# A fourth split buffer through the experts of a two-layer decoder trunk, with a new order for the last down tiles and the picks

## The reference

```python
logits = (ht @ w_router).astype(jnp.float32)
top_vals, top_idx = lax.top_k(logits, TOP_K)          # TOP_K = 2 of 8
top_w = jax.nn.softmax(top_vals, axis=-1)
...
for e in range(N_EXPERTS):
    y = swiglu(ht, w_gu[e], w_down[e], D_FF_EXPERT)    # D_FF_EXPERT = 1792
    out = out + combine[:, e:e + 1] * y.astype(jnp.float32)
```

## Time and profile before

| | us |
|---|---|
| median of 3 runs | 1234.74 |
| lowest and highest | 1233.70, 1234.78 |
| the profiled execution, its own time | 1234.06 |
| its span in the trace | 1232.2 |
| PE busy | 1213.9 (99%) |
| DVE busy | 899.6 (73%) |
| ACT busy | 721.4 (59%) |
| mean granted PE clock | 0.994 |

### The profile page before, as it was taken

One profiled execution on the slowest core, in us unless ns is written; L12 is line 12 of the kernel. 1 busy time (PEld: TensorE's weight loads), 2 busy tenths in 40 slices (PEclk: granted clock), 3 DMA queues, 4 the chain that ended last, 5 costly groups with the idle time before them and its releaser, 6 DMA issues.

```text
span 1232.2 us, 15422 instructions
## 1 busy us (share of the span) xinstructions
PE 1213.9 (99%) x6004; PEld 1012.5 (82%) x6004; DVE 899.6 (73%) x864; ACT 721.4 (59%) x677; POOL 110.7 (9%) x131
## 2 busy tenths in 40 slices
PE   9999999999999999999999999999999999999997
PEld 7997787788888888998788878888888888888876
DVE  5777755654544467667756668999898888888996
ACT  5346544534343446435644377777777777777765
POOL 4600000200000001330000100000010001000301
PEclk9999999999999999999999899999999999999999
DMA  9955454655555546655445389999999999999970
GB/s 299 318 172 171 139 181 158 232 179 198 178 198 179 198 153 212 190 169 177 155 167 185 137 296 373 373 385 378 386 382 380 388 384 384 382 390 379 391 280 35
DMA packets 152204, 317.55 MB, mean 258 GB/s; under 512 B 6273, under 2 KB 41345, under 8 KB 152146
## 3 DMA queue, kind: packets, MB, share of 16 engines
q1 hardware_dynamic: 147328, 302.27, 69.9%
q0 software_dynamic: 4112, 13.44, 3.0%
q10 hardware_dynamic: 706, 1.07, 0.3%
HBM read 310.99 MB, written 5.77 MB: 257 GB/s over the span
## 4 chain that ended last, share of the span: by engine, by line
PE 89%; DVE 6%; ACT 3%; issue 2%; POOLq 0%; POOL 0%; ACTq 0%; DVEq 0%
PE ps L1804 23%; PE ps L1549 16%; PE ps L1551 16%; PE ps L1550 16%; PE ps L1791 11%; DVE split L975 2%; ACT split L629 2%; PE ps L1771 1%; PE ps L1565 1%; PE ps L1586 1%; PE ps L1639 1%; DVE hT L1007 1%; PE ps L1665 1%; PE ps L1760 1%; PE ps L1694 0%
## 5 line engine op out<-in xcount | busy, mean ns | idle before, releaser
L975 DVE TENSOR_TENSOR split<-raw,split 128x2048 fp32r<-128x2048 f32 x279 | 639.2, 2295 | 231.2 <-ACT split L629 228.5
L629 ACT ACTIVATE split<-raw 128x2048 fp32r<-128x2048 f32 x279 | 534.4, 1916 | 262.7 <-PE ps L1551 192.9
L1804 PE MATMUL ps<-split,br 128*128 128x512 f32 x1344 | 317.7, 393 | 1.5 <-DVE br L1097 1.0
L1804 PEld LDWEIGHTS ps<-split,br 128*128 128x128 f32 x1344 | 249.4, 188 | 56.2 <-issue 2.1
L1549 PE MATMUL ps<-split,hT 128*128 128x512 f32 (+1 forms) x600 | 235.4, 392 | 3.2 <-DVE hT L1007 1.9
L1551 PE MATMUL ps<-split,hT 128*128 128x512 f32 (+1 forms) x600 | 230.5, 384 | 0.0
L1550 PE MATMUL ps<-split,hT 128*128 128x512 f32 (+1 forms) x600 | 230.3, 384 | 0.0
L1791 PE MATMUL ps<-split,hT 128*128 128x512 f32 x672 | 159.6, 392 | 0.1
L1791 PEld LDWEIGHTS ps<-split,hT 128*128 128x128 f32 x672 | 124.8, 188 | 27.9 <-issue 1.6
L1549 PEld LDWEIGHTS ps<-split,hT 128*128 128x128 f32 x600 | 112.8, 188 | 29.0 <-DVE hT L1007 3.6
L1551 PEld LDWEIGHTS ps<-split,hT 128*128 128x128 f32 x600 | 112.7, 188 | 22.6
(11 more groups left out here) (267 smaller groups left out, 990.3 us busy)
## 6 DMA issues: line engine op xcount, KB each, us to landing
raw<-moe_w_gu_dram SPq DMA_DIRECT2D x96, 1024.0 KB
raw<-moe_w_down_dram SPq DMA_DIRECT2D x56, 1024.0 KB
raw<-w_in_dram SPq DMA_DIRECT2D x45, 1024.0 KB
raw<-ffn_w_gu_dram SPq DMA_DIRECT2D x28, 1024.0 KB
raw<-moe_w_gu_dram SPq DMA_DIRECT2D x32, 512.0 KB
raw<-ffn_w_down_dram SPq DMA_DIRECT2D x14, 1024.0 KB
raw<-w_branch_dram SPq DMA_DIRECT2D x12, 1024.0 KB
raw<-w_out_dram SPq DMA_DIRECT2D x8, 1024.0 KB
```

The source lines that it names most:

```text
L629: act.activation(buffer(t, 0), raw[:, t % RAW, :], ACT.Copy).then_inc(hi, 1)
L975: dve.tensor_tensor(buffer(t, 1), raw[:, t % RAW, :], buffer(t, 0).bitcast(F32), ALU.subtract).then_inc(lo, 1)
L1804: ins = pe.matmul(ps[:, 5 if kind == "up" else 4, :], xe[:, sl, 4 * part + k, :], slot(t, sr, 512)[:, k, :], start=part + k + m == 0, stop ...
```

## The change

1. From the first tile of the embedding projection of layer 1 on (`LAST_RING`), the split ring has four buffers to the end; every fourth tile goes to the rows of `br`. Since 21 tiles are no multiple of 4, an expert's buffers are no longer those of the one before, and PE's loop over the experts is written out.
2. ACT and DVE split two tiles ahead as before up to step 9 of expert 1, two and three ahead in step 10 (`AT_AHEAD`), and three ahead from there. In step 18 of every expert, the split now stands behind the eviction of the tail.
3. The four picks go to four buffers (two of them the free `qT` and `kT`), issued one after the other; DVE adds them at steps 9, 10, 12, 13.
4. In the last expert the three last down tiles are taken first for output columns 0 to 511 and then for 512 to 1023; the turn of the tail comes after the first six matmuls. The first half is scattered and added (`add_last(b, 0)`) ahead of the second half's low part, which now lies in `pT`. The third and fourth turn of `X` stand later in `quad`.
5. `weight_exp` moves from expert 0 to the routing, followed by a small silu on ACT.

```diff
+LAST_RING = LAYER_T0[1] + T_PROJ[1]
-AT_COMBINE = (8, 9, 13, 14)
+AT_COMBINE = (9, 10, 12, 13)
+AT_AHEAD = (1, 10)
...
         def buffers(t):
-            return SPLIT + 1 if 0 <= t - LAYER_T0[1] < EXTRA else SPLIT
+            return SPLIT + 1 if 0 <= t - LAYER_T0[1] < EXTRA or t >= LAST_RING else SPLIT
...
+        def lead(i, j):
+            tiles = (2,) if (i, j) < AT_AHEAD else (2, 3) if (i, j) == AT_AHEAD else (3,)
+            return [n for n in tiles if i < EXPERTS - 1 or j + n < BODY_TILES]
...
             def picks(s):
+                pool.wait_ge(picked, s)
                 for n, (b, k) in enumerate(((0, 0), (0, 1), (1, 0), (1, 1))):
-                    if n < 2:
-                        pool.wait_ge(picked, s)
-                    else:
-                        pool.wait_ge(picks_used, 4 * (s - 1) + n - 1)
-                    pool.indirect_dma_start(Y[:, n % 2, :], None, ye_rows[s][:, :], bass.IndirectOffsetOnAxis(
+                    pool.indirect_dma_start(pick_rows[n], None, ye_rows[s][:, :], bass.IndirectOffsetOnAxis(
...
             def expert(s, t0, i, last):          # ACT; DVE alike
-                    if not last or j + 2 < BODY_TILES:
-                        split_hi(t0 + j + 2, i, BODY_TILES, s)
-                    if s == 1 and i == 0 and j == 1:
-                        weight_exp()
+                    elif j != AT_LAST:
+                        for ahead in lead(i, j):
+                            split_hi(t0 + j + ahead, i, BODY_TILES)
...
                     if j == AT_LAST:
                         ...
                         if not last:
                             gather_hi(s, 1, 2 + i * 2)
+                        if s == 1:
+                            for ahead in lead(i, j):
+                                split_hi(t0 + j + ahead, i, BODY_TILES)
+                            if last:
+                                split_gate_hi(0)
...
                     store_y(1)
+                    weight_exp()
                     proj_out_of(1, 0)
...
                 if last and s == 1:              # DVE
                     for nh in range(2):
                         dve.wait_ge(ye_hi, nh + 1)
+                        dve.tensor_tensor(ye[nh][:, 1, :], ps[:, nh, :], ye[nh][:, 0, :].bitcast(F32),
                                           ALU.subtract).then_inc(ye_lo, 1)
+                        if nh == 0:
+                            add_last(0, 0)
+                            add_last(1, 0)
...
-                    add_last(0, 0)
-                    add_last(1, 0)
+                    turn_lo(7, (0, 1))
                     add_last(0, 1)
-                    turn_lo(7, (0,))
                     add_last(1, 1)
-                    turn_lo(7, (1,))
                     split_gate_lo(1)
...
+                def last_downs():                # PE
+                    pe.wait_ge(aT_lo[1], LAST_F + i * (LAST_F + 1))
+                    down_half(AT_LAST, 2, 0, 0)
+                    turn_act(1, LAST_F, i, True)
+                    pe.wait_ge(lo, t0 + AT_LAST + 2 + i * BODY_TILES)
+                    down_half(AT_LAST + 1, 2, 1, 0)
+                    pe.wait_ge(aT_lo[1], LAST_F + 1 + i * (LAST_F + 1))
+                    pe.wait_ge(lo, t0 + AT_LAST + 3 + i * BODY_TILES)
+                    down_half(AT_LAST + 2, LAST_F, 0, 0).then_inc(half_down[1], 1)
+                    for n in range(3):
+                        down_half(AT_LAST + n, 2 if n < 2 else LAST_F, n % 2, 1).then_inc(used, 1)
...
-                with pe.Fori(0, EXPERTS - 1) as e:
-                    expert(s, t0, e, False)
+                if s == 1:
+                    for e in range(EXPERTS - 1):
+                        expert(s, t0, e, False)
...
                 expert(s, t0, EXPERTS - 1, True)
+                if s == 1:
+                    pe.wait_ge(ye_lo, 1)
+                    for b in range(NB):
+                        scatter(b, 0)
...
                 if l:
                     last_turn(0, 1)
+                    pe.wait_ge(ye_lo, 2)
+                    for b in range(NB):
+                        scatter(b, 1)
...
-                     {(0, 0, 0, 0): lambda: last_turn(2), (0, 0, 1, 1): lambda: last_turn(3)} if l else
+                     {(0, 0, 1, 1): lambda: last_turn(2), (0, 1, 0, 1): lambda: last_turn(3)} if l else
```

More of the change, by code:

```diff
@@ L1156, in expert @@
                                           aT_moe[:, 0].bitcast(F32), ALU.subtract).then_inc(aT_lo[s], 1)
-                    if not last or j + 2 < BODY_TILES:
-                        split_lo(t0 + j + 2, i, BODY_TILES, s)
-                    elif s == 1 and j + 2 == BODY_TILES:
-                        split_gate_lo(0)
+                    if s == 2:
+                        if not last or j + 2 < BODY_TILES:
+                            split_lo(t0 + j + 2, i, BODY_TILES, s)
+                    elif j != AT_LAST:
+                        for ahead in lead(i, j):
+                            split_lo(t0 + j + ahead, i, BODY_TILES)
                     if s == 1 and i == 1 and j == AT_WEIGHTS[0]:
@@ L1172, in expert @@
                             gather_lo(s, 1, 2 + i * 2)
+                        if s == 1:
+                            for ahead in lead(i, j):
+                                split_lo(t0 + j + ahead, i, BODY_TILES)
+                            if last:
+                                split_gate_lo(0)
                     if last and s == 1 and j in AT_COMBINE:
@@ L1777, in expert, with tile, down_half @@
                 _, _, lo, used = STREAMS[s]
+                def tile(j, s_, n):
+                    return slot(t0 + j + (i * BODY_TILES if s == 1 else 0), s_, n)
+                def down_half(j, f, part, nh):
+                    for k in range(2):
+                        for m, (sl, sr) in enumerate(((0, 0), (0, 1), (1, 0))):
+                            lhs = aT_moe[:, sl, 2 * part + k, :] if f < LAST_F else aT_tail[:, sl, k, :]
+                            ins = pe.matmul(ps[:, nh, :], lhs, tile(j, sr, D)[:, k, cols(nh)],
+                                            start=f + part + k + m == 0, stop=f == LAST_F and k == 1 and m == 2)
+                    return ins
+                def last_downs():
[9 more added lines that the diff above has]
+                        down_half(AT_LAST + n, 2 if n < 2 else LAST_F, n % 2, 1).then_inc(used, 1)
                 for j, (kind, f, part) in enumerate(EXPERT_TILES):
@@ L1780, in expert @@
                     pe.wait_ge(lo, t + 1 + i * BODY_TILES)
+                    if last and s == 1 and j == AT_LAST:
+                        last_downs()
+                        break
                     if kind == "down":
@@ L1787, in expert @@
                         for nh in range(2):
[L1788 to L1794 removed]
+                            ins = down_half(j, f, part, nh)
                             if f == LAST_F and nh == 0:
```

61 lines of the change are left out of this document (30 added, 31 removed).

## The result

The changed kernel takes 1237.97 us at the median of 10 runs (1235.38 to 1240.71), the kernel before 1232.88 in the 10 runs that now stand beside it (1230.22 to 1234.78). The ratio is 1.0039 [1.0029, 1.0049]: slower by 0.4%, some 4.8 us. The forecast of 1237.0 and its range hold the time, but the sum behind it was +2.3, so half of the loss was not in it. That the total came so near is in part luck: it was built on a median of 1234.74 from three runs, and the ten runs of the same kernel give 1232.88. From there +2.3 would have given 1235.2. The profiled execution takes 1237.28 us, its span 1235.4.

A forecast was written before the change was run, and what follows sets the result against it. It took PE, busy 99% of the span, as the bound, with DVE the engine PE waits for. Terms -1.7 + 2.5 + 0.4 + 1.2 gave +2.3 unrounded, on 1234.7: 1237.0 us, range 1231.2 to 1239.5.

The forecast's parts named there:

- Exponentials, -1.7: Expert 0: without the exponentials and table loads, PE's turn of step 4 no longer waits for DVE; 1.7 us gained.
- Step 18, +2.5: Expert 0: tile 20 is split behind the tail's eviction, so PE stands once for 2.5 us, not regained.
- The forecast: Whole kernel: the case in which the summed terms hold, 1237.0 us, own range 1235.8 to 1238.3; chance 0.50.
- the rival of the falling clock: Expert 0: clock falls in the 2.5 us stand, +2.5 to +5, 1239.5 to 1242 us; chance 0.12.
- Lead three, four buffers, 0: Experts 1 to 6: no PE stall to lose in 2 to 6, expert 1 even; 0, from -0.8 to +0.5.
- the rival of the loop boundaries: PE's expert boundaries: unrolling gains at most 0.4 us each, 7 x 0.4 = 2.8, time 1234.2; chance 0.04.
- Expert 7, 0: Expert 7: DVE bounds, stalls at tiles 12 to 17 return at tile 18, picks cost nothing; 0, from -1.1.
- the rival in which DVE does not bound: Experts 1 and 7: the buffer takes their stalls and the last turn does not wait; -1.0, 1233.7 us; chance 0.14.
- I leave it out of the sum: DMA transfers: the same bytes move and no ACT wait that was read ends at a transfer, so no term.
- Last down tiles, +1.36 and -1.0: End of expert 7: matmuls end 1.36 us later, `quad` starts 1.0 earlier relative to them; +0.4 in all.
- Turns later in `quad`, +1.2: `quad`: the later fourth turn delays gate tile 2, PE stalls 1.5 us against 0.3; +1.2.
- three signs of being wrong: Tile 20 of expert 0 not waited for, DVE idle in expert 7's second half, clock below 1.00 between 713 and 1224.

The follow-up runs named there:

- experiment 12: Changed kernel with tile 20 of expert 0 split ahead of the tail's eviction, old last down tiles and turns, old two-buffer picks: ratio 0.9977 to the kernel before.
- experiment 11: Changed kernel with tile 20 of expert 0 split ahead of the tail's eviction, and last down tiles, scatters and turns as before: ratio 0.9987 to the kernel before.
- experiment 2: Changed kernel with two unused f32 matmuls on PE between tiles 19 and 20 of expert 0: ratio 1.0023 to the kernel before.
- experiment 5: Changed kernel with tile 20 of expert 0 split ahead of the tail's eviction, and all twelve matmuls of tile 18 ahead of the tail's turn: ratio 1.0009.
- experiment 7: Changed kernel with tile 20 of expert 0 split ahead of the tail's eviction, and gate tile 2 split ahead of the fourth turned block: ratio 0.9987.
- experiments 1: Changed kernel with the split of tile 20 in expert 0 back ahead of the tail's eviction: ratio 1.0006 to the kernel before.
- experiment 4: The changed kernel run once more as it is, on the chip of three other runs: ratio 1.0031 to the kernel before, median 1237.72 us.
- experiment 6: Changed kernel with tile 20 of expert 0 split ahead of the tail's eviction, third and fourth gather issued after the first and second pick are added: ratio 1.0017.
- experiments 8: Changed kernel with tile 20 of expert 0 split early, tile 18 whole ahead of the tail's turn, later gathers held back, gate tile 2 split earlier: ratio 1.0015.
- experiment 9: Kernel before with only PE's experts 0 to 6 of the first expert layer written out in place of a loop: ratio 0.9996.
- 10: Changed kernel with tile 20 of expert 0 split early, gate tile 2 split ahead of the fourth turned block, picks in two buffers as before: ratio 0.9980.
- experiments 3: Kernel before with only the exponentials and the silu behind them moved to the routing: ratio 0.9991.

## Why the prediction was right, and where it was not

**Exponentials, -1.7: right.** 1.64 at the turn in the profile of after, 1.68 when they are moved alone. (The prediction's "61.77, so 1.9 over" took the end of the last matmul for the end of the expert; from start to start expert 0 is 1.7 over.)

**Step 18, +2.5: right as a stand (2.32), wrong as a price.** The stand was foreseen with its place and cause. "The forecast" took it as the whole price; the rival of the falling clock, with 0.12, was what happened, in both profiles of this kernel. The sentence that failed is "the stand is 0.4 shorter than the one that shows a fall". It took the moment when the clock drops behind the last matmul as the length of pause that it needs. In after the clock drops when PE works again, after a shorter pause: the drop comes up to 3.5 us after PE has stopped, so its moment says little of how short a pause is enough. It also failed in size: low for three to four microseconds and not five to ten, so +1.7 and not +2.5 to +5. The page "TensorE: Matmul & The Clock Gate" of the Trainium skill (HAM oscillation — how this bites in real kernels) describes such falls from pauses between bursts. These traces agree that a fall follows, and show it behind pauses shorter than those of the page's example, 2.32 us twice.

**Lead three, four buffers, 0: right for the buffers.** From expert 0's start to the rows turned, experiment 12 is at 407.40, 2.32 less than before. Moving the exponentials alone gives 1.68 and writing out PE's experts alone 0.71, together 2.39. Nothing is left that the fourth buffer could have given. The 0.13 in each steady expert is the loop's, the rival of the loop boundaries, at 0.12 a pass and not 0.4. The rule of the Trainium skill on instruction fetch ("Runtime: NRT & Kernel Launch", Instruction fetch mechanics) has its sign right here, at a size that the medians can't show; that a fetch is behind it is not shown.

**Expert 7, 0: right that DVE is the bound, wrong that picks cost nothing.** With the old picks the fourth buffer leaves tile 18 where it was, 64.16 and 64.23 against 64.31, as forecast; that falsifies the rival in which DVE does not bound. With the new picks tile 18 comes at 64.60 to 64.88, 0.4 to 0.7 later than in experiment 12, and 65.14 in the profile of after. The step that failed is "in the new order it is caught up at the same place (step 7) and has none after". In all nine kernels with the new picks DVE then waits 0.34 to 0.35 for ACT's next split, and ACT had waited for PE. With the old picks the first addition, at step 8, fills this wait; the change moved it to step 9. In experiment 11 that is nearly the whole difference to experiment 12 (0.44): behind it DVE never idles before the eviction of step 17, though ACT waits six times for weight tiles. The rest is the first of the late tiles, where it reaches DVE: 0.57 in after, 0.33 in experiments 2 and 5, 0.24 in experiment 7, at most 0.1 in experiments 1, 4 and 11. So "I leave it out of the sum" of the transfers failed too, for a smaller part: DMA is at a share of 1.04 in the steady experts, and behind four gathers of 0.5 MB in a row a weight tile comes late. To hold two of them back (experiment 6) takes the late tile from DVE, but not the 0.35, and the third pick is then 1.64 late at step 12. No kernel moved the steps alone; that the 0.35 is theirs is read from DVE's list and its waits.

**Last down tiles, +1.36 and -1.0: the first mis-sized, the second did not come.** PE stands 0.81 to 0.84 ahead of the turn, not 1.3, and tile 18 to scatter grows by 0.6 to 0.7, not 1.36, where the clock holds (1.2 in the profile of after, where it fell). The gain of 1.0 up to `quad` should have come from earlier turns of X. With the old end, the first turn of X starts 0.80 to 0.81 behind the start of DVE's first addition in each of five profiles, which is the addition itself and a hand-over. With the new end it starts 1.8 (after, experiment 2), 2.0, 2.2, 2.3, 2.4, 2.7 and 3.0 behind it, and only in experiment 6 again 0.80, where `quad` then starts 3.76 behind the scatter, so a whole microsecond sooner, as forecast. The trace names "DVE X" as releaser in most of these, but X was ready a microsecond and more before; in experiments 5 and 8 it says "issue". PE itself is late. What it waits for shows among the transfers. The queue q8 brings PE's instructions: only PE's list grew in experiment 9, and q8 grew with it (the pages of the kernel before and of experiment 9):

```profile
q8 instruction: 36, 0.59, 0.2%
q8 instruction: 49, 0.80, 0.3%
```

The table has the transfer of q8 nearest to the first scatter, in us from that scatter's start (negative is ahead of it). X is ready 0.80 behind the start of DVE's first addition.

| kernel | low part of the first half done | fetch starts | fetch lands | X ready | turn of X starts |
|---|---|---|---|---|---|
| after | -1.35 | -0.28 | 0.97 | 1.46 | 2.45 |
| 1 | -1.04 | 0.03 | 1.32 | 1.46 | 2.83 |
| 2 | -1.06 | 0.01 | 0.94 | 1.46 | 2.43 |
| 4 | -1.03 | 0.03 | 1.15 | 1.46 | 2.64 |
| 5 | -0.05 | 1.04 | 2.40 | 1.57 | 3.81 |
| 6 | -2.64 | -1.57 | -0.40 | 1.47 | 1.47 |
| 7 | -1.07 | 0.00 | 1.44 | 1.46 | 3.05 |
| 8 | -0.06 | 1.06 | 2.04 | 1.58 | 3.49 |
| 10 | -1.04 | 0.02 | 1.35 | 1.46 | 2.96 |

In all nine a fetch starts 1.06 to 1.12 behind DVE's low part of the first half, for which the scatter waits in PE's list, and in the eight late ones the turn starts 1.4 to 1.6 behind the landing. In experiment 6 the low clock held the scatter up, the fetch had landed before it, and nothing is late. With the old end (before, experiments 3, 9, 11 and 12) a fetch has landed 1.5 us or more ahead of the scatter, and the turn starts as soon as X is ready. So PE is late because its instructions are, and the sum had no such term. The two misses are of opposite sign and cancel in part: from tile 18 to `quad` the forecast was +0.4, and where the clock holds it measures +0.3 to +1.0 (experiments 1, 2, 4, 7 and 10), in after +0.9.

Why the fetch comes there is argued. Between the first scatter and the turn stands PE's branch around the second set of experts, which the change has moved from before the first scatter to behind it. With the old end PE had passed it in time: the scatter waits 0.25 for DVE's low part, 0.20 in experiment 11, and for nothing else. The Trainium skill's rule on taken branches (the section named above) would give such a fetch; no kernel here moved the branch alone. The prediction's 5.33 from the matmuls to `quad` counts their end at 0.227 each, 1196.05; the row has it at 1196.35, so 5.03.

**Turns later in `quad`, +1.2: right.** The stand is 1.33, the whole term 1.37 to 1.39, and taking gate tile 2 ahead gives it back.

The sum by steps: -1.64 + 2.32 + 1.73 (clock) - 0.59 (what is left up to expert 6, the loop) + 0.83 + 1.18 - 0.26 + 1.39 = +4.96, the +5.0 between the traces. By the bound of 2.5 us that the prediction set itself, slower came; it had "same" at 0.46 as the likeliest and "slower" at 0.36. Of its three signs of being wrong two came true: DVE idles in the second half of expert 7 (0.35 and 0.57), and the clock is below 1.00 at 772 and 1189. A forecast of +2.3 so near to the bound of 0.2%, with a stand in it that was next to the length of a known clock fall, should have leaned to slower: the clock's price belonged into the sum with more than 0.12.

## What to carry to other kernels

When an edit opens a stand of about two microseconds on a busy PE, count it nearly double until the trace shows that the clock holds, and remember that an exception for the first pass (a lead of two that is three later) must keep the old place of its instruction. When an engine that bounds a stretch gets its work in a new order, walk its waits as well as its work: a step that filled a wait costs nothing where it was, and its moving opens the wait. Where DMA runs at a share near 1, a larger read-ahead of one stream is taken from another: look for the stream whose consumer then waits. Where an engine starts late with its data ready, look at its instruction queue among the transfers; a fetch that is hidden under queued matmuls shows once it falls into a short dependent chain.

## What the runs showed of the hardware

- From the start of the experts to the last matmul, PE stood for more than 1.1 us in 29 places of the fourteen profiles. All four stands of 2.28 to 2.62 us were followed by a clock at half (2.32 in after and experiment 4, 2.28 and 2.62 ahead of the turn of X in experiments 8 and 5), of the seven of 1.81 to 2.08 three (2.05 in after, 2.08 in experiment 6, 1.81 in experiment 5, but not 2.04, 1.97, 1.88 and another 1.81), of the eighteen up to 1.74 none. With 1.88 us of f32 matmuls in a stand of this kind, the rest 0.60, the clock held (one profile). The drop came 2.2 to 3.5 us after PE had stopped, in six of the seven with PE at work again, and lasted between 3 and 4 us, in experiment 6 nearly 7. In experiment 6 the windows show it at half, with PE at work again:

```profile
1185.00:1187.00 2.00, 1.23 (x6) 0.71 (x5) 1.61 (x2) 0.00 (x0) 0.00 (x0) 0.67 0.87 346
1187.00:1189.00 2.00, 2.00 (x7) 1.62 (x6) 0.43 (x1) 1.61 (x3) 0.00 (x0) 0.50 0.08 31
```

- PE's first turn behind a fetch of its instructions (16 KB, 0.9 to 1.4 us) came 1.0 to 2.2 us later than its data in eight profiles, 1.4 to 1.6 us behind the landing, and on time in one in which the fetch was early. The profile's releaser names the data or "issue", not the fetch.
- Kernels that differ by nothing ahead of the experts begin expert 0 anywhere from 710.1 to 714.5 (experiments 1 and 5). Sums between events of the same trace are worth more here than single executions' totals.
